# Attention of the running streams moved into the input projection, with cached keys turned as 32x32 blocks

## What is computed

```
h = rms_norm(x, norm_w)                       # 1024 + 128 rows, 1024 wide
u = h @ w_in                                  # 1024 x 6144: q k v gate | q k v gate | merge gates A, B
qd, kd = rope(qd), rope(kd)
# A: differential attention, 4 heads, q1 q2 k1 k2 of 64 and v of 128
p = softmax(where(mask, q k^T / 8, -1e30));  w = p[0] - lam * p[1];  o_da = w v
# B: stick-breaking attention, 8 heads of 64
z = q k^T / 8
after = reverse_cumsum(log_sigmoid(-z)) - log_sigmoid(-z)
o_sb = exp(log_sigmoid(z) + after) v          # strictly causal
merged = sigmoid(ga) * (y_da @ w_proj_da) + sigmoid(gb) * (y_sb @ w_proj_sb)
x = x + merged @ w_out
```

## Time and profile before

| | |
|---|---|
| median of three runs | 3607.6 us |
| span of the profiled execution (its own time, first to last instruction) | 3607.5 us |
| TensorE (PE) busy | 3153.7 us, 87% |
| VectorE (DVE) busy | 1565.5 us, 43% |
| ScalarE (ACT) busy | 1003.8 us, 28% |
| DMA | 516.62 MB, 143 GB/s in the mean |
| projection stages | 39.8 to 637 us, 1821 to 2418 us |
| attention stages | 637 to 1543 us, 2418 to 3317 us |
| merge stages | 1543 to 1789.6 us, 3317 to 3575 us |

### The profile page before, as it was taken

How to read it: one execution, slowest core, us unless ns; L and a number is a source line. 1 busy time by engine, 2 the same in 40 slices (tenths; PEclk the granted TensorE clock), 3 DMA queues, 4 the chain that set the end, 5 groups by cost and what they waited for, 6 DMA issues and landing times. The chain is left out here.

```text
span 3607.5 us, 52841 instructions
## 1 busy us (share of the span) xinstructions
PE 3153.7 (87%) x19664; PEld 2367.0 (66%) x19664; DVE 1565.5 (43%) x2399; ACT 1003.8 (28%) x1751; POOL 0.2 (0%) x4
## 2 busy tenths in 40 slices
PE   6999999788888888869889999988888888886896
PEld 4888888455565555658678888875555555555685
DVE  4522200454564555655263121005645547355643
ACT  3001111343433434321030011114424344342211
POOL 0000000000000000000000000000000000000000
PEclk9999999888988889979989999999889899898898
DMA  4322221655554554354242222117455544552534
GB/s 170 137 96 93 81 87 47 219 197 175 166 170 147 195 181 145 122 194 140 94 147 100 94 93 96 73 69 242 166 176 179 198 162 150 177 180 92 191 129 162
DMA packets 288645, 516.62 MB, mean 143 GB/s; under 512 B 19040, under 2 KB 89824, under 8 KB 282208
## 3 DMA queue, kind: packets, MB, share of 16 engines
q1 hardware_dynamic: 288432, 513.72, 41.2%
HBM read 433.43 MB, written 84.93 MB: 144 GB/s over the span
## 5 line engine op out<-in xcount | busy, mean ns | idle before, releaser
L185 PE MATMUL A_acc<-A_w_hi,A_ht_hi 128*128 128x512 f32 x1728 | 676.2, 391 | 5.9 <-DVE A_w_lo L326 5.9
L185 PE MATMUL A_acc<-A_w_hi,A_ht_lo 128*128 128x512 f32 x1728 | 674.5, 390 | 0.0
L185 PE MATMUL A_acc<-A_w_lo,A_ht_hi 128*128 128x512 f32 x1728 | 674.3, 390 | 0.0
L185 PEld LDWEIGHTS A_acc<-A_w_hi,A_ht_hi 128*128 128x128 f32 x1728 | 325.7, 189 | 73.9 <-issue 6.6
L718 PE MATMUL B_tr<-ident,B_k 128*128 128x128 f32 x2048 | 335.8, 301 | 43.4 <-DVE B_ckt L948 27.3
L185 PEld LDWEIGHTS A_acc<-A_w_hi,A_ht_lo 128*128 128x128 f32 x1728 | 325.6, 188 | 68.2
L185 PEld LDWEIGHTS A_acc<-A_w_lo,A_ht_hi 128*128 128x128 f32 x1728 | 325.9, 189 | 67.3
L774 PE MATMUL B_sc<-B_kt,B_qt 64*128 64x512 f32 (+3 forms) x768 | 343.2, 556 | 7.7 <-DVE B_kt L948 7.7
L718 PEld LDWEIGHTS B_tr<-ident,B_k 128*128 128x128 f32 x2048 | 240.7, 152 | 162.4 <-issue 59.5
L948 DVE COPY B_ckt<-B_tr 128x512 f32<-128x512 f32 x272 | 186.8, 687 | 138.7 <-PE B_tr L718 138.1
L795 PE MATMUL B_ov<-B_nat_v,B_wt 128*128 128x64 f32 (+1 forms) x1728 | 231.1, 290 | 0.0
(11 more groups left out here) (140 smaller groups left out, 3611.5 us busy)
## 6 DMA issues: line engine op xcount, KB each, us to landing
B_k<-in_cache_da_k SPq DMA_DIRECT2D x64, 1024.0 KB, 5.3
B_v<-in_cache_da_v SPq DMA_DIRECT2D x64, 1024.0 KB, 9.6
B_k<-in_cache_sb_k SPq DMA_DIRECT2D x64, 1024.0 KB, 5.3
B_v<-in_cache_sb_v SPq DMA_DIRECT2D x64, 1024.0 KB, 9.6
A_w_raw<-in_w_in SPq DMA_DIRECT2D x48, 1024.0 KB, 5.5
tmp_gates<-A_stage SPq DMA_DIRECT2D x72, 256.0 KB, 2.0
D_gate<-tmp_gates SPq DMA_DIRECT2D x72, 256.0 KB, 3.8
D_w_raw<-in_w_merge SPq DMA_DIRECT2D x32, 512.0 KB, 6.0
```

The source lines that it names most:

```text
L185: last = nc.tensor.matmul(acc[:, i % RING, :], h[:, k, t * P:(t + 1) * P], w[:, b, k, :], start=(n == 0), stop=(n == 3 * KC - 1))
```

## The change

The sample attention leaves the attention stage and goes into the projection stage. There are 16 items in a layer: 8 streams in differential attention, then the same 8 in stick-breaking attention.

A new function `project_plan()` gives every step of the projection stage a position, in units of one group, and sorts them; all engines walk the sorted list. Item s starts at 17.4 + 4.6 s groups for the first eight, and every 6.2 groups for the others.

```
+    starts = [17.4 + 4.6 * s for s in range(DEC_BATCH)]
+    starts += [starts[-1] + 4.6 + 6.2 * s for s in range(DEC_BATCH)]
+    for n in range(NBLK * NT):
+        for p in range(WP):
+            at(n + p / WP, "mm", n, p)
+        at(n + 1.05, "evac", n)
+        at(n + 1.30, "store", n)
...
+    for s, base in enumerate(starts):
+        da = s < DEC_BATCH
+        length, lag, gap = (4.6, 1.6, 0.6) if da else (6.2, 2.5, 0.8)
+        prev = starts[s - 1] if s else 0.0
+        at(prev + 0.35 if s else -3.0, "load_k", s)
+        for piece in range(NPIECE):
+            at(12.0 + piece if s == 0 else prev + 1.35 + piece * (base - prev - 2.0) / NPIECE, "key_t", s, piece)
+        at(11.5 if s == 0 else prev - 0.5, "load_q", s)
+        at(base - 0.6, "query_t", s)
+        at(base, "scores", s)
+        at(base + 0.05, "new_scores", s)
...
+        at(base + 0.55, "functions", s)
+        if not da:
+            at(base + 1.1, "scan", s)
+        first = base + lag
+        for r in range(PVR):
+            at(first + r * gap, "prob_t", s, r)
+            at(first + r * gap + 0.2, "prob_take", s, r)
+            at(first + r * gap + 0.5, "values", s, r)
...
+        at(first + gap + 0.55, "load_v", s, 3)
+        at(first + 2 * gap + 0.55, "load_v", s, 4)
+        if s + 1 < ITEMS_S:
+            at(first + 0.55, "load_vn", s + 1)
+            at(first + 3 * gap + 0.55, "load_v", s + 1, 1)
+            at(first + 4 * gap + 0.55, "load_v", s + 1, 2)
```

Keys aren't turned by TensorE any more. VectorE turns each 32x32 block of a piece in place, and the scores are 64 matmuls of 32x32 tiles that add up over four 32-wide quarters d of the head's dimensions; row group b takes the keys whose frame lies in its 32 partitions, and has its own PSUM bank:

```
+                        keys = kt[:, s * PIECE:(s + 1) * PIECE, :].rearrange("p j c -> p (j c)")
+                        nc.vector.transpose(keys, keys).then_inc(S["key_turned"], 1)
...
+                        for d in range(4):
+                            for b in range(4):
+                                for c in range(NC):
+                                    o = (c * 4 + d) * 32
+                                    quad = slice(32 * b, 32 * b + 32)
+                                    last = nc.tensor.matmul(csc[32 * c:32 * c + 32, b, :], qkt[quad, 0, o:o + 32], kt[quad, :, o:o + 32],
+                                                            start=(d == 0), stop=(d == 3))
```

Buffers of the projection shrink:

```
-RING = 6
+WSLOTS = 5
+TILES = [NT - 1] + list(range(NP_T))
...
-        w_raw = sbuf("A_w_raw", [P, 2, KC // 2 * BLK])
-        w_hi = sbuf("A_w_hi", [P, 2, KC, BLK], F32R)
-        stage = sbuf("A_stage", [P, RING, BLK])
+        w_raw = sbuf("A_w_raw", [P, 2, 2 * BLK])
+        w_hi = sbuf("A_w_hi", [P, WSLOTS, 2 * BLK], F32R)
+        stage = sbuf("A_stage", [P, 2, BLK])
+        kt = sbuf("A_kt", [P, KT, BLK])
+        v_in = sbuf("A_v", [P, 2, PIECE, BLK])
...
-        acc = psum("A_acc", [P, RING, BLK])
+        acc = psum("A_acc", [P, 2, BLK])
+        csc = psum("A_csc", [P, NPIECE, BLK])
```

More of the change, by code:

```diff
@@ L116, in _ @@
             def _(sp):
-                def load_w(blk, first):
-                    for half in range(2):
-                        if not first:
-                            sp.wait_ge(S["w_lo_done"], 2 * blk + half - 1)
-                        sp.dma_start(w_raw[:, half, :], dram["w_in"][l, blk, half]).then_inc(w_sems[half], 16)
-                def store(pair, i):
-                    sp.wait_ge(S["psum_free"], pair * GROUPS + i + 1)
-                sp.dma_start(nw[:, :], dram["norm_w"][l]).then_inc(S["consts_in"], 16)
@@ L165, in _ @@
+                for s in range(2):
+                    sp.wait_ge(stored[s], 16 * (NBLK * NT // 2))
+                sp.wait_ge(S["co_stored"], 16 * NC * ITEMS_S)
             @block.tensor
             def _(pe):
-                def transposes(t):
-                    pe.wait_ge(S["hn_ready"], t + 1)
-                    if t >= 1:
-                        pe.wait_ge(S["ht_lo"], 2 * t)
-                    for half in range(2):
-                        for k in range(HALF):
-                            last = nc.tensor.transpose(tr[:, half, k * P:(k + 1) * P],
-                                                       hn[:, (half * HALF + k) * P:(half * HALF + k + 1) * P], ident[:, :])
-                        last.then_inc(S["ht_tr"], 1)
@@ L178, in product @@
-                def product(base, i, t, b, first_pair):
-                    if not (first_pair and i < RING):
-                        pe.wait_ge(S["psum_free"], base + i - RING + 1)
-                    n = 0
-                    for k in range(KC):
-                        for h, w in ((ht_hi, w_hi), (ht_hi, w_lo), (ht_lo, w_hi)):
-                            last = nc.tensor.matmul(acc[:, i % RING, :], h[:, k, t * P:(t + 1) * P], w[:, b, k, :],
-                                                    start=(n == 0), stop=(n == 3 * KC - 1))
-                            n += 1
-                    last.then_inc(S["mm_done"], 1)
@@ L430, in slice_in @@
         return [(rounds, "slice_t", a, which, half) for which in range(2) for half in range(2)]
-    def sample_probs(i):
-        return [(rounds, "c_prob_t", i, j) for j in range(KT // 4, -1, -1)]
-    def sample_values(i):
-        return [(add, "c_values", i, s) for s in range(NPIECE)]
     def scores(n, m):
@@ L1054, in phase_merge @@
 def phase_merge(nc, l, dram, const):
[L1057 removed]
+    scope, sbuf, psum = open_scope(nc, l)
     D = D_MODEL
@@ L1415, in _ @@
                     sp.dma_start(const[name][:, :], dram["c_" + name]).then_inc(const["loaded"], 16)
-        with nc.Fori(0, DEPTH) as l:
+        for l in range(DEPTH):
             phase_project(nc, l, dram, const)
```

955 lines of the change are left out of this document (438 added, 517 removed).

## The result

The changed kernel takes 3457.9 us (median of 4 runs, 3454.0 to 3463.1) against 3606.4 before (4 runs, 3600.7 to 3625.1): a ratio of 0.959, interval 0.955 to 0.963. It is faster by 149 us, where 344 had been forecast.

What follows compares the result with a forecast made beforehand. TensorE was taken to bound the kernel, without a gap in the projection stage. A layer: +203 + 50 + 18 - 439 - 4 = -172, two layers -344, so 3607.5 - 344 = 3263, stated as 3262 us; range 3080 to 3530.

Steps and rivals of the forecast that it cites:

- start: Before the projection's first matmul: 4 MB of keys and other loads queued ahead delay it, +18 us a layer.
- items: Projection stage: the sample's scores, values and weight turning on TensorE, 12.7 us for each of 16, +203 us a layer.
- stalls: Projection stage: TensorE waiting for split weights, cached values and PSUM evacuation, +50 us a layer, ends zero and 100.
- entry: Entry of the attention stage: loses the turning of the sample's queries and two memsets, -4 us a layer.
- attention passes: Attention stage: four passes at 113 us, 452 in place of 891.5, -439 us a layer.
- merge: Merge stage: claimed to stay the same, so no change in the sum.
- a pass is 107 to 127.7, I take 113: Attention stage: 127.7 us if only the sample's busy time goes, less 14.3 of waits the sample makes.
- The lower end: Attention stage: 107 us a pass, the prompt's own TensorE work if no wait stays.
- The prompt alone can't fill TensorE: Attention stage: small query blocks leave a third of the prompt's work at 1.2 GHz; 143 us a pass, 3502; chance 0.10.
- Row tiles queue: Projection stage: the 64 score tiles run four at a time, +10.3 us an item, +330, 3592, no change; chance 0.07.
- Key turns on VectorE: Projection stage: four 2048-element pieces an item at 2.29 us each, 147 us a layer, covered by TensorE.
- Transfers bind: Projection stage: loads and stores set its time, 1118 us at 172 GB/s, +250 a layer, 3762, slower; chance 0.07.

Runs made afterwards that it cites:

- The turns put back: Changed kernel plus 256 transposes of a constant a pass on TensorE, which nothing waits for: 3448.0 us, ratio 0.956.
- full rows: Changed kernel with the prompt's score matmuls contracting over 128 rows instead of 64, zeros in the other component's rows: 3233.9 us, ratio 0.896.
- wide values: Changed kernel with each value matmul of the second (stick-breaking) kind streaming 128 columns instead of 64: 3323.6 us, ratio 0.922.
- no items: Changed kernel with all sample work left out of the projection stage, its attention rows stored as zeros: 2922.4 us in one run.
- keys later: Changed kernel with the first item's 4 MB of keys issued at position 6 instead of ahead of the first x tile: 3421.6 us, ratio 0.946.

## Why the prediction was right in direction and wrong in size

A layer, from the starts and windows above (layer 0; the start from layer 1):

| term | forecast | measured | off by |
|---|---|---|---|
| start | +18 | +6 (48.6 for 39.8 in layer 0: +9) | -12 |
| projection stage, items, stalls, entry | +203 + 50 - 4 = +249 | 880.5 - 611.7 = +269 | +20 |
| attention passes | -439 | 535 - 891.5 = -356.5 | +82 |
| merge | 0 | 252.5 - 246.6 = +6 | +6 |
| sum | -172 | -76 | +96 |

Twice -76 is near the 146 us by which the profiled span fell.

- **The step that failed: "a pass is 107 to 127.7, I take 113".** It was 133.7, above my upper end. Both ends took the prompt's durations from the kernel before, at the clock that the mixture of prompt and sample had. I took the half-clock stretches of before as given ("every half-clock stretch stays") when they grew from some 51 to 86 us a pass. The two waits that I took out did go: TensorE waits for little now. The turns put back show the cause, full rows and wide values the price: with the clock held, a pass is 100.3 us, below my lower end.
- **The lower end was no bound either.** The busy times of the earlier trace rows overlap where one tile's matmuls begin before another's end: the six tiles add up to 380.6 + 400.3 = 780.9 us, where TensorE is busy 751.9 in the four passes of the earlier trace rows. And the slices of queries and keys are 32 transposes a pass, not 64, at some 0.2 us each; that leaves their 7 us as they were.
- **The rival that held.** "The prompt alone can't fill TensorE" named a clock below 0.8 and 143 us a pass, 3502; measured 0.68, 133.7 and 3458. That 3458 lies in the range of 3080 to 3530 is due to this rival; the forecast's own range ended at 3400. (The terms that I listed for it, +118 and +100, add up to 3480.) I gave the rival 0.10, since "the passes' mean clock is still 0.85 to 0.90". That mean was made in part by the very work that was to leave, so it could not speak for what stays. Its reason was off as well: the cold stretches are not small blocks that wait for other engines, but the middle blocks of the first kind and the large ones of the second, in which TensorE is busy for 30.00 of 30 and 48.14 of 51 us.
- **Items on TensorE, +203:** measured +217 of busy time (no items). Scores 4.45 us for 3.4; the rest, 9.1 us, is within 0.2 of its sum. The 868 us that I named for the stage held the start's 18 too; the 873.0 measured begin after it, so that they are close is luck. The Trainium skill, page "TensorE: Matmul & The Clock Gate", section "Part 3: Packing small matmuls — row/col tiling", gave 10.6 times for 16 tiles, 5.1 us by the estimate then (the sum by it is 3317, not 3315); measured 64 x 0.85 / 4.45 = 12 times.
- **"Row tiles queue"** is refuted by the 4.45 us. Its price was +330; even with the row groups one after the other it is half of that, 3622 - 3458 = +164.
- **Stalls, +50:** 52.2 us idle in the stage, but in other places. The weights at block boundaries, where I put 44, wait 9.4. More than half of that is a split behind a scan on VectorE, which I had feared for PSUM only. Instead 13.8 are the new values of the first item: their load waits for a store that stands behind 4 MB of keys, and I had followed the queue for weights and cached values only. The turned weights of the cached values cost 9.7, those of the new values 5.1.
- **Start, +18:** +9 and +6. The direction was right (keys later takes it back), the 14 us for 5.2 MB ahead of the norm were too many.
- **Key turns on VectorE:** 2.30 us where I took 2.29; TensorE never waits for one. The Trainium skill, page "Vector Engine (DVE) Microarchitecture Reference", section 3.8, led to 2.1; the measurement is 8% above it.
- **"Transfers bind":** the stage moves 217 GB/s, and TensorE waits for no load of the cache itself. Weights land in 4.6 us where the earlier trace rows had 6.0 for the merge's.

## What to carry to other kernels

Before work is struck out of a busy engine, look at the granted clock of what would remain by itself: a busy share of 100% at 0.50 is half a pace, and durations read from a mixture hold only for the mixture. Where matmuls are cheap in use of the array (half the rows, few columns per weight load), try the same number of them with all rows or more columns before anything else; here two such edits gave 258 us on the changed kernel and 111 on the one before, for the 149 of the restructuring. And follow the small dependent loads of a new schedule through the in-order queue, with the stores that they wait for, not only the large ones.

## What the runs showed of the hardware that I had not expected

- TensorE stayed near 1.2 GHz for 30 us while the profile had it busy without a gap, and a pass whose scores went over 128 rows ran at a mean clock of 0.84 for 0.68.
- 256 added transposes a pass cost nothing (3448 for 3458 us), 64 added matmuls of 400 columns a pass gained 40 us, and doubling the columns of 288 value matmuls a stage (576 instructions) gained 134.
- The same score matmul took 878, 674 and 633 ns where the pass had a mean clock of 0.68, 0.85 and 0.93, all over 64 rows; over 128 rows, at 0.93, it took 631.
- 64 score tiles of 32x32 over 512 columns take 4.45 us with neighbours in different row groups, and 9.14 us row group by row group.
